# Routing table by 0/1 products and weights by gathers without repeats in the expert stage of a one-core layer kernel

## The chip, the core and the metric

The kernel runs on one core of one Trainium2 chip. The metric is the device time in microseconds of one execution, lower is better. The engines of a core are TensorE (PE; its weight loads are PEld), VectorE (DVE), ScalarE (ACT), GpSimd (POOL) and SyncE (SP, which here only issues DMAs). Each has its own instruction queue, and semaphores tie them together. Sixteen DMA engines serve the transfers that SP, ACT and POOL issue.

## What is computed

One layer of a hybrid backbone: modulated norm, two token mixers (mLSTM and gated linear attention) on one input projection, a gated merge, and then a mixture of experts over the 1024 latent tokens of width 1024. The change touches the mixture of experts and one line of the first stage. Cut to that part, the reference is:

```python
def hier_moe(h, w_grp, b_grp, w_rexp, b_rexp, w_up, w_down):
    p_grp = softmax(hf @ w_grp + b_grp); grp_p, grp = top_k(p_grp, 1)          # 4 groups
    e_logits = (hf @ w_rexp + b_rexp).reshape(n_tok, 4, 4)
    p_in = softmax(e_logits[arange(n_tok), grp[:, 0]]); top_p, top_i = top_k(p_in, 2)
    weights = grp_p * top_p / sum(top_p)
    expert = grp * 4 + top_i                                                   # 2 of 16 experts a token
    # assignments sorted by expert, each expert's segment padded to 128 rows
    ...
    def expert_block(xb, e):                                                   # xb: 128 x 1024
        gate, up = split(xb @ w_up[e], 2)                                      # w_up[e]: 1024 x (512 + 512)
        return (silu(gate) * up) @ w_down[e]                                   # w_down[e]: 512 x 1024
    # y[token] += weight * row
```

All arithmetic is float32; the kernel reaches that precision by splitting each operand into a high part in float32r and a low part, and forming three products (high x high, high x low, low x high). Two choices of 1024 tokens are 2048 assignments, padded to at most 31 blocks of 128 rows (BLOCKS = 31), always all computed; blocks that no expert needs use expert 15's weights.

## The kernel before

The program runs stages one after the other; each stage is a block of instructions for the five engines that ends when all of them have. The last four are `mix_out` (projections, second norm, router logits), `route`, `experts` and `combine`.

`route` is mostly one chain on VectorE in which each operation waits for the one before (`then`). It waits for the router's bias (loaded by SP at its start), finds group and experts, their weights, and the place of each assignment: `dest_i`, block x 128 + rank. TensorE helps with two products for prefix sums. From the token counts it derives the number of blocks of each expert (L2296 to L2298) and the expert of each block, `block_e` (L2302 to L2305). Last it computes `place_i`, where each assignment's token number belongs in a table in DRAM, `row_token` (L2318 to L2320), which SP has filled with zeros.

`experts` begins on GpSimd with 16 scatters of 128 words into that table (L2401), its load back into SBUF (L2405), and from there one gather of 128 rows of x for each block (L2414), whose indices are copied from the table first (L2411). SP meanwhile loads the weights: for each block three pieces of 2 MB, piece 0 the gate half of `w_up` (512 of its 1024 columns), piece 1 the up half, piece 2 `w_down`. The expert is read from `block_e` into a register, and all 31 blocks load all three. Each piece has one buffer in `ex_raw`, free when its low part is done.

For every block, ScalarE copies a piece to its high part `ex_w_hi` in two halves (L2477) and VectorE subtracts to get `ex_w_lo` (L2517), both one block ahead for pieces 0 and 1. TensorE multiplies the block's x (transposed by L2433, split by L2481 and L2522) with piece 0 into `ex_g_ps` and with piece 1 into `ex_u_ps` (L2424 to L2426, 24 products each), transposes the next x, does the down product of the block before, and transposes the hidden values (L2464). ScalarE's Silu is L2495, VectorE's gate product L2532, the hidden halves L2539 and L2541; ScalarE empties the down product (L2487) and stores it (L2489). The loop over blocks is a hardware loop over pairs, with the first two and the last written out.

The contraction runs over `(k p)`: chunk k of 128 takes x columns 128k to 128k+127.

`combine` gathers the two rows of each token and adds them. It is not touched.

## Time and profile before

| | us |
|---|---|
| median of 3 runs | 2668.78 (2663.82 to 2674.18) |
| the profiled execution, whole | 2670.58 |
| its span, first to last instruction | 2668.6 |
| routing, first to last VectorE operation | 1914.33 to 1931.98 |
| first expert product on TensorE | 1968.95 |
| Silu of first and of last block | 1976.8, 2570.2 |
| combine, to the end | 2601.8 to 2668.6 |

All times in the rows are microseconds from the start of the span, in one profiled execution. A row of the timeline gives the start, the duration, the engine, the line of the kernel, the operation with output and inputs, how many instructions were merged in it (x8), and in brackets how long the engine had been idle before it and who released it. A duration of a single matmul includes its way through the array; how fast products follow each other is seen from their starts.

### The profile page before, as it was taken

Reading aid. Unit: us, or ns where it says so; the run is one execution under the profiler, and the core shown is the slowest. Engines: PE = TensorE matmul, PEld = TensorE weight load, DVE = VectorE, ACT = ScalarE, POOL = GpSimd, SP = SyncE. Lnnn points to the kernel's source line nnn. Section 1 sums busy time; section 2 is a strip of 40 time slices with the busy share of each in tenths; the row PEclk is TensorE's granted clock in tenths of the full one; section 3 lists DMA queues with packets and bytes.
Section 4 is the critical chain, followed back from the end, with each engine's and each line's share of the span. In section 5 each row is a group of like instructions: output and inputs, shape, how many; then the busy total and the mean of one; then the engine's idle time right before and its main releaser. Section 6 shows DMA issues by size and latency. Waiting matters only on the chain. (4 is left out here: it accounts for less than half of the span.)

```text
span 2668.6 us, 28745 instructions
## 1 busy us (share of the span) xinstructions
PE 2264.5 (85%) x10734; PEld 1822.7 (68%) x10734; DVE 1417.7 (53%) x1723; ACT 1053.4 (39%) x1302; POOL 773.0 (29%) x571
## 2 busy tenths in 40 slices
PE   6989979993999995799999689999349999999970
PEld 1278868872888884688888567777337777777760
DVE  1435631104323222779887445433348888888856
ACT  1322201111234333354554434422136666766643
POOL 5300001000346443466766322200132112111105
PEclk9989989995999996899999889999569999999995
DMA  7633252113444555233354466552279999999956
GB/s 274 216 74 91 74 199 86 49 48 135 130 143 143 142 141 164 75 125 113 118 134 114 126 212 193 179 161 84 75 272 360 373 377 360 374 371 359 374 192 267
DMA packets 325269, 500.12 MB, mean 187 GB/s; under 512 B 22102, under 2 KB 171750, under 8 KB 324524
## 3 DMA queue, kind: packets, MB, share of 16 engines
q1 hardware_dynamic: 306156, 433.65, 48.0%
q0 software_dynamic: 12816, 43.55, 5.5%
q10 hardware_dynamic: 6192, 21.51, 2.0%
q8 instruction: 68, 1.11, 0.2%
q14 instruction: 37, 0.30, 0.0%
HBM read 409.96 MB, written 88.69 MB: 187 GB/s over the span
## 5 line engine op out<-in xcount | busy, mean ns | idle before, releaser
L2517 DVE TENSOR_TENSOR ex_w_lo<-ex_raw,ex_w_hi 128x2048 fp32r<-128x2048 f32 x186 | 417.8, 2288 | 115.3 <-ACT ex_w_hi L2477 113.3
L2477 ACT ACTIVATE ex_w_hi<-ex_raw 128x2048 fp32r<-128x2048 f32 x186 | 345.8, 1908 | 92.0 <-DMA ex_raw<-in_w_up_dram 51.8
L666 POOL DMA_DIRECT2D vals<-rows_stage x40 | 21.8, 546 | 438.8 <-ACT rows_stage L658 438.8
L2411 POOL COPY ex_idx<-ex_rows 128x1 int32 (+1 forms) x31 | 20.9, 675 | 434.6 <-PE ex_x_ps L2433 433.1
L2424 PE MATMUL ex_g_ps<-ex_w_hi,ex_x_hi 128*128 128x512 f32 x248 | 104.5, 422 | 42.6 <-DVE ex_x_lo L2522 42.6
L1527 PEld LDWEIGHTS gl_lv_ps<-gl_q_level,gl_k_level 128*128 128x128 f32 x896 | 108.3, 194 | 10.5 <-issue 5.6
L1992 DVE TENSOR_TENSOR mo_w_lo<-mo_w,mo_w_hi 128x1024 fp32r<-128x1024 f32 x48 | 59.8, 1245 | 100.7 <-ACT mo_w_hi L1889 100.7
L878 PE MATMUL gl_u_ps<-half_hi,gl_u_w_hi 128*128 128x512 f32 x256 | 110.3, 431 | 3.4 <-ACT gl_u_exp L896 3.4
L1527 PE MATMUL gl_lv_ps<-gl_q_level,gl_k_level 128*128 128x64 f32 x896 | 111.0, 276 | 2.3 <-DVE gl_scores L1657 1.5
L2103 PE MATMUL mo_ps<-mo_branch_hi,mo_w_hi 128*128 128x512 f32 x256 | 105.4, 412 | 6.4 <-DVE mo_w_lo L1992 5.9
L878 PE MATMUL ml_u_ps<-half_hi,ml_u_w_hi 128*128 128x512 f32 x256 | 104.0, 406 | 8.0 <-ACT ml_u_exp L896 8.0
L658 ACT ACTIVATE rows_stage<-rows_ps 128x512 f32<-128x512 f32 x40 | 23.9, 598 | 211.7 <-PE rows_ps L635 211.7
L2424 PE MATMUL ex_y_ps<-ex_w_hi,ex_hidden_hi 128*128 128x512 f32 x248 | 100.7, 406 | 7.6 <-DVE ex_w_lo L2517 7.6
L879 PE MATMUL gl_u_ps<-half_lo,gl_u_w_hi 128*128 128x512 f32 x256 | 103.5, 404 | 0.0
L2104 PE MATMUL mo_ps<-mo_branch_hi,mo_w_lo 128*128 128x512 f32 x256 | 103.2, 403 | 0.0
L880 PE MATMUL gl_u_ps<-half_hi,gl_u_w_lo 128*128 128x512 f32 x256 | 103.1, 403 | 0.0
L2105 PE MATMUL mo_ps<-mo_branch_lo,mo_w_hi 128*128 128x512 f32 x256 | 102.8, 402 | 0.0
L879 PE MATMUL ml_u_ps<-half_lo,ml_u_w_hi 128*128 128x512 f32 x256 | 101.5, 396 | 0.0
L2425 PE MATMUL ex_g_ps<-ex_w_lo,ex_x_hi 128*128 128x512 f32 x248 | 101.3, 409 | 0.0
L880 PE MATMUL ml_u_ps<-half_hi,ml_u_w_lo 128*128 128x512 f32 x256 | 101.3, 396 | 0.0
L2426 PE MATMUL ex_g_ps<-ex_w_hi,ex_x_lo 128*128 128x512 f32 x248 | 101.1, 408 | 0.0
L2426 PE MATMUL ex_y_ps<-ex_w_hi,ex_hidden_lo 128*128 128x512 f32 x248 | 99.6, 402 | 0.0
(378 smaller groups left out, 6181.6 us busy)
## 6 DMA issues: line engine op xcount, KB each, us to landing
ex_raw<-in_w_up_dram SPq DMA_DIRECT2D x62, 2048.0 KB, 12.7
ex_raw<-in_w_down_dram SPq DMA_DIRECT2D x31, 2048.0 KB, 9.9
fr_w<-in_w_mod_dram SPq DMA_DIRECT2D x12, 2048.0 KB, 10.0
ml_u_w<-in_w_in_dram SPq DMA_DIRECT2D x32, 512.0 KB, 5.6
gl_u_w<-in_w_in_dram SPq DMA_DIRECT2D x32, 512.0 KB, 5.1
expert_rows<-ex_y ACTq DMA_DIRECT2D x31, 512.0 KB, 7.4
vals<-rows_stage POOLq DMA_DIRECT2D x40, 256.0 KB, 2.3
ml_v<-vals SPq DMA_DIRECT2D x20, 512.0 KB, 3.9
```

Source lines behind the costliest of these rows:

```text
L878: pe.matmul(self.ps[:, :], a_hi, b_hi, start=(k == 0), stop=False)
L879: pe.matmul(self.ps[:, :], a_hi, b_lo, start=False, stop=False)
L880: last = pe.matmul(self.ps[:, :], a_lo, b_hi, start=False, stop=(k == KD - 1))
L1527: last = pe.matmul(lv_ps[at_l // 2 % 2][:, lv_cols(at_l, h)], kl[:, d, l, h * P:(h + 1) * P], ql[:, l, h * P // 2:(h + 1) * P // 2], start ...
L2103: pe.matmul(out, a_hi, b_hi_, start=(k == 0), stop=False)
L2104: pe.matmul(out, a_lo, b_hi_, start=False, stop=False)
L2105: last = pe.matmul(out, a_hi, b_lo_, start=False, stop=(k == KD - 1))
L2424: pe.matmul(dst, a_hi[:, ka], hi[:, q, at:at + 512], start=first, stop=False)
L2425: pe.matmul(dst, a_hi[:, ka], lo[:, q, at:at + 512], start=False, stop=False)
L2426: return pe.matmul(dst, a_lo[:, ka], hi[:, q, at:at + 512], start=False, stop=last)
L2477: act.activation(hi[:, q, h], raw[:, q, h], ACT.Copy).then_inc(hi_done[q], 1)
L2517: dve.tensor_tensor(lo[:, q, at], raw[:, q, at], hi[:, q, at].bitcast(F32), ALU.subtract)\
```

## The change

It has four parts.

The table. `route` keeps `dest_i`, but instead of a table in DRAM it builds it in SBUF: for each of the two choices and each of 8 columns of tokens it forms two 0/1 tiles, `rt_is_rank` (128 tokens x 128 ranks) and `rt_in_block` (128 tokens x 32 blocks, times the token number), and 16 products in one accumulation give `m.table`, rank x block. The scatters, their table in DRAM and `place_i` are gone. Each expert now has at least one block, so that block 0 is always expert 0's. The number of blocks comes from an add and a shift. The router bias is loaded in the first stage, `constants`.

The first block. Since it is expert 0's, SP loads its three pieces at the start of `route`, and ScalarE makes the high halves of pieces 0 and 1 there. The weight buffers are placed before `route` for that.

The gathers. All later weights are fetched by GpSimd's indirect DMA, with one row of 16 KB per partition. The row numbers `m.w_rows` hold, for each block and piece, expert x 256 + 2 x partition (+ 1) or expert x 128 + partition; where the expert is that of the block before, 2^20 is added, which is outside the bound and is skipped, so that `ex_raw` keeps what it has. The splitting into high and low parts is done for every block as before.

The pieces. A gathered row holds whole rows of the matrix, so piece 0 is now the first 4 of each 8 rows of `w_up` with all 1024 columns (gate and up), piece 1 the other 4. Each piece feeds both `ex_g_ps` and `ex_u_ps`, and the gate is complete when 36 of 48 products are done (`g_made`). x is transposed by columns that lie 8 apart and the hidden values by columns 4 apart. ScalarE splits piece 0 ahead of the Silu, and makes `ex_x_hi` ahead of piece 1; VectorE makes `ex_x_lo` ahead of piece 1. The loop is written out for all 31 blocks.

```diff
-            then(ts(blocks[:, :], pre[:, N, :], 0.0, None, ALU.is_gt))
-            for q in range(1, SEQ // P):
-                then(dve.scalar_tensor_tensor(out=blocks[:, :], in0=pre[:, N, :], scalar=float(P * q),
-                                              in1=blocks[:, :], op0=ALU.is_gt, op1=ALU.add))
+            then(ts(count_i[:, :], pre[:, N, :], float(P - 1), None, ALU.add))
+            then(ts(count_i[:, :], count_i[:, :], 7, None, ALU.logical_shift_right))
+            then(ts(blocks[:, :], count_i[:, :], 1.0, None, ALU.max))
...
+            up = w["w_up"][0][0].rearrange("(p h k) n -> h p (k n)", h=2, k=KD // 2)
+            down = w["w_down"][0][0].rearrange("(p k) n -> p (k n)", k=FF // P)
+            for q, src in enumerate((up[0], up[1], down)):
+                sp.dma_start(raw[:, q, :], src).then_inc(first[q], 16)
+            sp.wait_ge(first[2], 16)
...
+            for k in range(TOP_K):
+                pe.wait_ge(places, k + 1)
+                for n in range(N):
+                    last = pe.matmul(table_ps[:, :], is_rank[:, k, n, :], in_block[:, k, n, :],
+                                     start=(k == 0 and n == 0), stop=(k == TOP_K - 1 and n == N - 1))
+            last.then_inc(tables, 1)
...
+            then(ts(where_i[:, 0], m.dest_i[:, :, :], P - 1, None, ALU.bitwise_and))
+            then(ts(where_i[:, 1], m.dest_i[:, :, :], 7, None, ALU.logical_shift_right))
+            then(dve.tensor_copy(where[:, :, :, :], where_i[:, :, :, :]))
...
+            for k in range(TOP_K):
+                then(tt(hit[:, k], wide(where[:, 1, k, :], WIDE), along(which[:, :], WIDE), ALU.is_equal))
+                then(tt(in_block[:, k], hit[:, k], wide(token[:, :], WIDE), ALU.mult))
+                tt(is_rank[:, k, :, :], wide(where[:, 0, k, :], P), along(rank[:, :], P), ALU.is_equal)\
+                    .then_inc(places, 1)
+            dve.wait_ge(tables, 1)
+            then(dve.tensor_copy(m.table[:, :], table_ps[:, 0:BLOCKS]))
...
+            then(tt(again[:, 1:], blk[:, 1:], blk[:, 0:BLOCKS - 1], ALU.is_equal))
+            then(ts(again[:, :], again[:, :], float(SKIP), None, ALU.mult))
+            for q, rows in enumerate((2 * P, 2 * P, P)):
+                if q != 1:
+                    then(dve.scalar_tensor_tensor(out=row0[:, :], in0=blk[:, :], scalar=float(rows), in1=again[:, :],
+                                                  op0=ALU.mult, op1=ALU.add))
+                then(ts(m.w_rows[:, q, :], row0[:, :], part[:, q:q + 1], None, ALU.add))
...
-            def load(b, q):
-                e = sp.value_load(m.block_e[0:1, bass.ds(b, 1)], min_val=0, max_val=EXPERTS - 1)
...
+                pool.wait_ge(lo_done[q], 2 * b)
+                rows = EXPERTS * P * (1 if q == 2 else 2)
+                pool.indirect_dma_start(out=raw[:, q, :], out_offset=None, in_=sources[q],
+                                        in_offset=bass.IndirectOffsetOnAxis(ap=m.w_rows[:, q, b:b + 1], axis=0),
+                                        bounds_check=rows - 1, oob_is_err=False).then_inc(loaded[q], 16)
...
+                by_chunk = xg[:, j, :].rearrange("p (c k) -> p k c", k=KD)
                 for k in range(KD):
-                    last = pe.transpose(x_ps[:, k * P:(k + 1) * P], xg[:, j, k * P:(k + 1) * P], m.ident[:, :])
+                    last = pe.transpose(x_ps[:, k * P:(k + 1) * P], by_chunk[:, k, :], m.ident[:, :])
...
             def step(b, j, half):
-                act.wait_ge(made[0], b + 1)
+                if more(b):
+                    split_hi(b + 1, 0)
+                act.wait_ge(s["g_made"], b + 1)
...
                 if more(b):
-                    split_hi(b + 1, 0)
+                    x_hi(b + 1)
                     split_hi(b + 1, 1)
-                    x_hi(b + 1)
...
                 if more(b):
+                    x_lo(b + 1)
                     split_lo(b + 1, 1)
-                    x_lo(b + 1)
```

How instructions stand on an engine, in the words of the built programs (line, operation, output from inputs, shape, how many in a row). First VectorE in one block of the expert stage, before:

```order
L2517 TENSOR_TENSOR ex_w_lo<-ex_raw,ex_w_hi 128x2048 x4
L2532 TENSOR_TENSOR ex_hidden<-ex_u_ps,ex_gate 128x512
L2517 TENSOR_TENSOR ex_w_lo<-ex_raw,ex_w_hi 128x2048 x2
L2522 TENSOR_TENSOR ex_x_lo<-ex_x_ps,ex_x_hi 128x1024
L2539 CAST ex_hidden_hi<-ex_h_ps 128x512
L2541 TENSOR_TENSOR ex_hidden_lo<-ex_h_ps,ex_hidden_hi 128x512
```

And after; of the four subtractions in the first row, two are the third piece of the block before and two the first piece of the next block:

```order
L2549 TENSOR_TENSOR ex_w_lo<-ex_raw,ex_w_hi 128x2048 x4
L2564 TENSOR_TENSOR ex_hidden<-ex_u_ps,ex_gate 128x512
L2554 TENSOR_TENSOR ex_x_lo<-ex_x_ps,ex_x_hi 128x1024
L2549 TENSOR_TENSOR ex_w_lo<-ex_raw,ex_w_hi 128x2048 x2
L2571 CAST ex_hidden_hi<-ex_h_ps 128x512
L2573 TENSOR_TENSOR ex_hidden_lo<-ex_h_ps,ex_hidden_hi 128x512
```

The low half of x has moved ahead of the subtraction of the second piece. Next ScalarE in one block, before, from the Silu on:

```order
L2495 ACTIVATE ex_gate<-ex_g_ps 128x512
L2477 ACTIVATE ex_w_hi<-ex_raw 128x2048 x4
L2481 ACTIVATE ex_x_hi<-ex_x_ps 128x1024
L2487 ACTIVATE ex_y<-ex_y_ps 128x1024
L2489 DMA expert_rows<-ex_y 128x1024
L2477 ACTIVATE ex_w_hi<-ex_raw 128x2048 x2
```

And after:

```order
L2530 ACTIVATE ex_gate<-ex_g_ps 128x512
L2514 ACTIVATE ex_x_hi<-ex_x_ps 128x1024
L2510 ACTIVATE ex_w_hi<-ex_raw 128x2048 x2
L2520 ACTIVATE ex_y<-ex_y_ps 128x1024
L2522 DMA expert_rows<-ex_y 128x1024
L2510 ACTIVATE ex_w_hi<-ex_raw 128x2048 x4
```

The first piece's high half now stands ahead of the Silu (the last two of the four at the end), and x between the Silu and the second piece. Last GpSimd, from the start of the expert stage, before:

```order
L2401 DMA row_token<-token,place_i 4096x1 x16
L2405 DMA ex_rows<-row_token 128x32
L2411 COPY ex_idx<-ex_rows 128x1
L2414 DMA ex_x<-moe_in,ex_idx 128x1024
L2411 COPY ex_idx<-ex_rows 128x1
L2414 DMA ex_x<-moe_in,ex_idx 128x1024
```

And after (the pattern of four repeats from there for each block):

```order
L2432 DMA ex_x<-moe_in,table 128x1024 x2
L2425 DMA ex_raw<-in_w_up_dram,w_rows 128x4096
L2425 DMA ex_raw<-in_w_up_dram,w_rows 128x4096
L2432 DMA ex_x<-moe_in,table 128x1024
L2425 DMA ex_raw<-in_w_up_dram,w_rows 128x4096
L2425 DMA ex_raw<-in_w_up_dram,w_rows 128x4096
L2425 DMA ex_raw<-in_w_down_dram,w_rows 128x4096
L2432 DMA ex_x<-moe_in,table 128x1024
```

The scatters and the copies of indices are gone, and the weight fetches, which SP issued before, stand in GpSimd's queue between the gathers of x.

## Rows read from the trace of the kernel before

**Rows 1.** The page, part 1: busy time of each engine, share of the span.
```profile
PE 2264.5 (85%) x10734; PEld 1822.7 (68%) x10734; DVE 1417.7 (53%) x1723; ACT 1053.4 (39%) x1302; POOL 773.0 (29%) x571
```

**Rows 2.** Stretches: length, busy of PE, PEld, DVE, ACT, POOL, clock, DMA share, GB/s.
```profile
2200.00:2300.00 100.00, 92.93 (x420) 74.62 (x419) 83.23 (x51) 68.89 (x46) 18.87 (x11) 0.98 0.99 366
```

**Rows 3.** Timeline, routing: start, duration, engine, line, operation, idle time before.
```profile
1911.62 0.43 SPq L2206 DMA_DIRECT2D rt_bias<-in_b_rexp_dram  x1
1914.33 0.33 DVE L2246 TENSOR_TENSOR rt_lg<-logits,rt_bias 128x160 f32<-128x160 f32 x1 [3.60 <-DMA rt_bias<-in_b_rexp_dram]
...
1925.90 1.43 DVE L2298 SCALAR_TENSOR_TENSOR rt_blocks<-rt_pre,rt_blocks 128x16 f32<-128x16 f32 x7
...
1927.59 0.68 DVE L2302 TENSOR_TENSOR rt_le<-rt_ends,rt_which 128x496 f32<-128x496 f32 x1
...
1931.81 0.17 DVE L2320 CUSTOM_DVE_ANT_0 place_i<-place_i,rt_hi 128x32 uint16<-128x32 uint16 x1
```

**Rows 4.** Timeline, start of the expert stage.
```profile
1933.23 1.11 POOL L2401 DMA_INDIRECT row_token<-token,place_i  x1 [21.50 <-POOLq L2164]
...
1954.22 0.96 POOL L2401 DMA_INDIRECT row_token<-token,place_i  x1 [0.30 <-issue]
...
1960.03 1.02 POOL L2414 DMA_INDIRECT ex_x<-moe_in,ex_idx  x1 [0.83 <-POOL ex_idx L2411]
...
1964.62 1.97 PE L2433 MATMUL ex_x_ps<-ident,ex_x 128*128 128x128 f32 x8 [41.16 <-DMA ex_x<-moe_in,ex_idx]
...
1967.68 1.22 DVE L2522 TENSOR_TENSOR ex_x_lo<-ex_x_ps,ex_x_hi 128x1024 fp32r<-128x1024 f32 x1 [19.65 <-ACT ex_x_hi L2481]
...
1968.95 0.80 PE L2424 MATMUL ex_g_ps<-ex_w_hi,ex_x_hi 128*128 128x512 f32 x1 [2.37 <-DVE ex_x_lo L2522]
```

**Rows 5.** The Silu of every block (L2495): all 31 in one row; then two neighbours.
```profile
L2495 ACT ACTIVATE ex_gate<-ex_g_ps x31: 598/598/602, 1976.8 to 2570.2; 128x512 f32<-128x512 f32 x31
...
1997.69 0.60 ACT L2495 ACTIVATE ex_gate<-ex_g_ps 128x512 f32<-128x512 f32 x1 [6.97 <-PE ex_g_ps L2426]
2016.96 0.60 ACT L2495 ACTIVATE ex_gate<-ex_g_ps 128x512 f32<-128x512 f32 x1 [1.96 <-PE ex_g_ps L2426]
```

**Rows 6.** Timeline of one block, TensorE, ScalarE and VectorE.
```profile
2214.60 0.39 PE L2424 MATMUL ex_u_ps<-ex_w_hi,ex_x_hi 128*128 128x512 f32 x1
...
2216.93 0.39 PE L2425 MATMUL ex_u_ps<-ex_w_lo,ex_x_hi 128*128 128x512 f32 x1
...
2220.20 1.04 PE L2433 MATMUL ex_x_ps<-ident,ex_x 128*128 128x128 f32 x8
2226.67 0.60 PE L2464 MATMUL ex_h_ps<-ident,ex_hidden 128*128 128x128 f32 x4
2228.16 0.49 PE L2424 MATMUL ex_g_ps<-ex_w_hi,ex_x_hi 128*128 128x512 f32 x1 [0.90 <-DVE ex_x_lo L2522]
...
2220.45 3.72 ACT L2477 ACTIVATE ex_w_hi<-ex_raw 128x2048 fp32r<-128x2048 f32 x2 [1.45 <-PE ex_u_ps L2426]
...
2226.82 1.22 DVE L2522 TENSOR_TENSOR ex_x_lo<-ex_x_ps,ex_x_hi 128x1024 fp32r<-128x1024 f32 x1
```

**Rows 7.** Timeline of the same block: GpSimd's gather and VectorE's subtractions beside it.
```profile
2222.55 2.98 POOL L2414 DMA_INDIRECT ex_x<-moe_in,ex_idx  x1 [0.79 <-POOL ex_idx L2411]
...
2222.40 4.49 DVE L2517 TENSOR_TENSOR ex_w_lo<-ex_raw,ex_w_hi 128x2048 fp32r<-128x2048 f32 x2
```

**Rows 8.** DMA, 2000 to 2500; then one weight load of 1936 to 1954 (us to landing).
```profile
DMA packets 72598, 184.35 MB, mean 369 GB/s; under 512 B 2000, under 2 KB 2000, under 8 KB 72595
...
ex_raw<-in_w_up_dram SPq DMA_DIRECT2D x50, 2048.0 KB, 13.0
...
ex_raw<-in_w_up_dram SPq DMA_DIRECT2D x1, 2048.0 KB, 7.9
```

**Rows 9.** Timeline, routing: two reductions, of elements 4 apart and of neighbours.
```profile
1916.90 0.37 DVE L2268 TENSOR_REDUCE rt_es<-rt_sel 128x32 f32<-128x128 f32 x1
...
1930.73 0.42 DVE L2315 TENSOR_REDUCE rt_dest<-rt_prod 128x16 f32<-128x256 f32 x1
```

More of the change, by code:

```diff
@@ L2351, in experts @@
         s = {name: sem(f"ex_{name}") for name in (
-            "table", "idx", "t_x", "x_hi", "x_lo", "gate", "hidden", "t_h", "h_hi", "h_lo", "y_left",
-            "gather_begun")}
-        loaded, hi_done, lo_done, made = ([sem(f"ex_{n}{q}") for q in range(3)] for n in (
-            "loaded", "hi_done", "lo_done", "made"))
-        scattered = sem("ex_scattered")
+            "t_x", "x_hi", "x_lo", "g_made", "gate", "hidden", "t_h", "h_hi", "h_lo", "y_left")}
+        loaded, made = ([sem(f"ex_{n}{q}") for q in range(3)] for n in ("loaded", "made"))
@@ L2365, in each @@
[L2365 to L2388 removed]
+            for b in range(BLOCKS):
+                body(b, b % 2, b // 2)
@@ new lines, in experts, with _, gather @@
+        late = lambda b, n: b >= n
+        more = lambda b: b < BLOCKS - 1
+        @block.gpsimd
+        def _(pool):
+            def load(b, q):
+                pool.wait_ge(lo_done[q], 2 * b)
[3 more added lines that the diff above has]
+                                        bounds_check=rows - 1, oob_is_err=False).then_inc(loaded[q], 16)
+            def gather(b):
+                if b >= 2:
+                    pool.wait_ge(s["t_x"], b - 1)
+                pool.indirect_dma_start(out=xg[:, b % 2, :], out_offset=None, in_=m.h2,
+                                        in_offset=bass.IndirectOffsetOnAxis(ap=table[:, b:b + 1], axis=0))\
+                    .then_inc(gathered[b % 2], 16)
+            gather(0)
+            gather(1)
+            for b in range(BLOCKS):
+                if b + 1 < BLOCKS:
@@ L2419, in _ @@
+                if b:
+                    load(b, 2)
+                if b + 2 < BLOCKS:
+                    gather(b + 2)
         @block.tensor
@@ L2735, in build @@
         if upto >= 4:
-            run(route, experts, combine)
+            with ExitStack() as moe:
+                m.ex_raw = place(moe, "ex_raw", [P, 3, KD // 2 * D])
+                m.ex_hi = place(moe, "ex_w_hi", [P, 3, KD // 2 * D], F32R)
+                m.ex_lo = place(moe, "ex_w_lo", [P, 3, KD // 2 * D], F32R)
+                run(route, experts)
+            run(combine)
 _INS = ["x", "c", "ctx", "c_ctx", "w_mod", "b_mod", "g_norm1", "w_in", "ml_conv", "ml_conv_b", "b_mgate", "ml_norm",
```

172 lines of the change are left out of this document (76 added, 96 removed).

## The prediction

> **What bounds the kernel now.** I read the page first: TensorE is busy 85% of the span, far ahead of VectorE's 53% [rows 1]. That average says little about the two stages that the change touches, so next came the stretches and the order of time inside them.
>
> The expert stage takes about 630 us. In a stretch of it TensorE is busy 93 us of 100, VectorE 83, ScalarE 69, and the 16 DMA engines show a share of 0.99 at 366 GB/s [rows 2]: everything is near its limit. Which wait ends last? The gate activations mark the blocks: the first at 1976.8, the last at 2570.2 [rows 5], 593.4 us for 30 steps, a mean of 19.78. The shortest step is 19.27 (1997.69 to 2016.96) [rows 5] and returns often. Its anatomy stands in [rows 6]: the gate and up products end when the transposes start at 2220.20; ScalarE then splits the second weight piece (3.72), VectorE subtracts behind it, and only at 2226.82 does it reach the low half of x (1.22), which TensorE waits for until 2228.16, idle 0.90 us. So 19.27 is a loop of dependences; TensorE alone would need less. What makes the mean 0.5 us longer is the weights: 75 weight loads of 2 MB and 25 blocks' rows in and out are 184.35 MB in 500 us, 369 GB/s [rows 8], 7.34 MB a block, which at that rate is 19.9 us. Two limits lie on each other.
>
> Ahead of it is a hole. VectorE starts routing at 1914.33 after a wait of 3.60 us for the bias [rows 3], ends it at 1931.98, and TensorE's first expert product starts at 1968.95 [rows 4]. Between them GpSimd issues 16 scatters of one word a row (1933.23 to 1955.2), loads the table, gathers x (1960.03), and x is transposed from 1964.62 [rows 4]. No weight is awaited there.
>
> **The change part by part.** *Start of the expert stage.* The bias is loaded in the first stage instead, so VectorE starts at about 1911.2: 3.1 off. The seven comparisons of 1.43 us and the first one become three small operations of some 0.21: 1.0 off. The three operations behind the destination go: 0.6 off. The expert of each block (from 1927.59, 1.6 us) moves behind the table [rows 3]. The destination is thus known at 1925.6 instead of 1931.35. Added: three small operations (0.6); for each of two choices two operations of 256 elements (0.43, between the 0.33 of 160 and the 0.68 of 496) and one of 1024 (1.22, as x_lo in [rows 4]), 4.2 in all; then 8 more products of 32 columns and their hand-off, 1.9 us (bounds 0.8 and 2.2); the table's copy, the block experts and seven small operations for the weight rows, 3.3. Routing ends at 1935.6. From the last routing operation to GpSimd's first took 1.25 us (1931.98 to 1933.23), so the gather of x is issued at 1936.9. Before, it was 4.6 us from issue to transpose (1960.03 to 1964.62) and 4.35 from there to the product [rows 4]. But now VectorE subtracts two SBUF tiles at that moment, and beside such a subtraction a gather took 2.98 us [rows 7] against 1.02 [rows 4]; I add 1.9. First product: 1936.9 + 6.5 + 4.35 = 1947.7, **21.2 us earlier** (19 to 23). The 6 MB of block 0 and the hi halves of its up pieces need about 18 us of DMA and 7.4 of ScalarE, hidden behind 24 us of routing; SP only waits there. Two more small loads on SP in the first stage come behind six others while TensorE still transposes: nothing, 0.5 at worst.
>
> *Less to load.* From the reference's inputs I worked out the tokens per expert: experts 0 to 7 and 12 to 15 have one block each, 8 to 11 have 3, 3, 4, 3. That is 25 blocks; the 6 unused ones repeat expert 15. So 15 of 31 blocks repeat the expert before and fetch no weights, and 16 do (block 0 in routing). A repeat needs 1.05 MB instead of 7.34, so DMA leaves its path. Of the 15 others, 8 (blocks 1 to 8) and 4 (21 to 24) follow each other and stay bound by DMA; 11, 14 and 18 stand alone, and a slot is free for some 12 us before it is needed, against 7.9 for one load that runs alone [rows 8] and 1 to 3 us of GpSimd: hidden.
>
> *x_lo ahead of the second piece.* The x halves need only the x transposes. TensorE's own work is 72 products at a start-to-start of 0.233 us (2214.60 to 2216.93 is ten) = 16.8, plus 1.04 and 0.60 for the transposes [rows 6]: 18.45. What is late next? The second piece is split while the first is multiplied: its low half is done 19.9 us after the products' start and needed at 18.45 + 5.6 = 24. VectorE's row (three pieces at 4.49 [rows 7], 1.22, three of 0.7) is 16.8 us in 18.45: I find 0.3 us of slack. With hand-offs 18.6.
>
> *Strided transposes.* Row halves need x columns 8 apart and hidden columns 4 apart. No TensorE row here reads columns apart. Bounds: zero, and the nearest row, on VectorE: a reduction of 128 elements that lie 4 apart took 0.37 us, one of 256 side by side 0.42 [rows 9]. With 0.16 of fixed cost that is 1.64 ns an element against 1.02, 1.6 times. A transpose takes 0.130 (1.04/8); 1.6 times 0.14 of load is +0.085. Twelve a block: 0 to +1.0 us. That row is another engine's, and the loading of one tile overlaps the passing of the last, so I take the middle, +0.5: pace 19.1.
>
> *Issue by GpSimd.* Four indirect DMAs a block at 1.0 to 3.0 us each are 4 to 12 us of GpSimd in 19. They are queued in one order: next block's two up pieces, this block's down, x. Behind a waiting load stand only loads that come free later, and x, which has over 10 us. A gather of 16 KB rows is not in this trace; skipped rows neither. I take 1 to 3 us for both.
>
> **The sum.** Block 0 to 1 has no down product before it: 13.2 (products: the gate came 7.6 after their start at half of them [rows 4, 5], plus 24 x 0.233) + 1.1 + 1.0 + 1.2 + hand-offs = 17.3. Eleven steps at DMA's pace, 19.8. Eighteen at 19.1. Together 17.3 + 217.8 + 343.8 = 578.9, against 593.4: **14.5 off**. The last block's tail and the combine stage stay. 21.2 + 14.5 = 35.7. The profiled execution had a span of 2668.6 within 2670.6 us; the new one 2632.9 within 2634.9. The median of the runs was 1.8 below the profiled one: **2633**.
>
> **The rivals.** *A, strides are free:* 18 steps at 18.6, 9 off more: 2624. For it: no TensorE row shows such a cost, and the next tile is loaded while the last one passes.
>
> *B, strides cost the full 0.085:* pace 19.6, 9 more than my sum, and 1 at the start: 2643. The Trainium skill speaks for it (Advanced Engine Details and Errata, SBUF Cachelines): a line is 16 bytes, and an access pattern that touches another line each time pays a penalty. It names no size for TensorE; by it both strided reads pay, and the time would be near 2643. VectorE's row agrees; no run here yet shows TensorE's.
>
> *C, GpSimd's issue makes loads late:* each slot is then free for 3 us less, and the eleven steps take 21.5: +19, 2652. For it: before, two loads were queued back to back and the queue never ran dry [rows 2, 8]. Against it: slots take 6.5 (split) + 3 + 7.9 = 17.4 under 19.8.
>
> *D, slower:* a fetch of rows four times as long costs GpSimd four times 0.96, and 2 to 2.7 of waiting for VectorE: about 6.5. Three and a gather are 22.5 us in every block, whether skipped or not, and GpSimd becomes the bound: 30 x 22.5 = 675, 81.6 more, minus 21.2: 2729. It turns into a loss from 20.5 us a block, 5.8 a fetch. Against it: a scatter of 128 words took as long (0.96) as a gather of 128 rows of 4 KB (1.02) [rows 4], so rows count and not bytes.
>
> The other direction of the same port: VectorE could be held by the four issues. The pair of subtractions beside the gather took 4.49, as any other [rows 7]. The Trainium skill (SBUF — State Buffer, SBUF: two separate sides) says that whoever of the two starts first holds the pair of ports for its whole instruction and the other fully blocks. By that rule VectorE would lose up to 1 us four times a block and the pace would be near 21; the row shows GpSimd waiting and VectorE not, so this stays inside D's chance.
>
> **How the numbers follow.** Forecast 0.35, A 0.27, B 0.20, C 0.10, D 0.08. The predicted time is 2633. D is left out of the range, and a tenth for the far ends; from A minus its uncertainties (start 2, the eleven steps faster by 1 us each if long rows load better) to C plus some: 2608 to 2658. A measurement of this kernel tells 0.5%, 13 us, from no change. Faster by more (below 2655.4): forecast, A, B and two thirds of C with a reserve, 0.84; within: 0.09; slower: 0.07.
>
> **What the profile of the changed kernel would show.** The first expert product 19 to 23 us earlier; no scatters. DMA share near 1 only in blocks 1 to 8 and about 21 to 24, low elsewhere, and some 101 MB of expert weights instead of 195. Steps between gates of 18.5 to 19.2 in repeats (18.6 says A, 19.6 B), eight x transposes in 1.04 (A) or up to 1.7 (B). x_lo ahead of the subtraction of the second piece, and TensorE's wait before a block's first product gone. GpSimd's issues at 1 to 3 us (D: 6). I would be wrong if TensorE waits for the first or second piece in repeats (VectorE's 0.3 us of slack gone), or for late weights in the first eight blocks.

## The result, and the profile after

| | before | after |
|---|---|---|
| median of 4 runs, us | 2671.48 (2663.82 to 2681.14) | 2597.13 (2587.59 to 2600.56) |
| ratio, 95% interval | | 0.9714 (0.9671 to 0.9758) |
| profiled execution: whole, span | 2670.6, 2668.6 | 2594.0, 2592.3 |
| first expert product of block 0 | 1968.95 | 1946.66 |
| first expert product of block 30 | 2564.33 | 2488.33 |
| mean step between blocks | 19.85 | 18.06 |

The change is 2.9% faster. The forecast was 2633 with a range from 2608 to 2658: the direction was right, and the time is 11 us below the range. The two spans differ by 76.3 us: 22.3 lie ahead of the first expert product, 53.7 in the 30 steps between blocks (595.38 against 541.67), and 0.3 behind them. Forecast were 21.2, 14.5 and 0, so the whole miss is in the steps. The DMA packets carry 94 MB less than the 500.12 MB of before, as forecast (101 MB of expert weights in place of 195).

The page of after, part 1 (busy time, share of the span, instructions), and the total of the DMA packets. They answer [rows 1]:

```profile
PE 2247.4 (87%) x10750; PEld 1827.3 (70%) x10750; DVE 1417.2 (55%) x1732; ACT 1051.2 (41%) x1302; POOL 815.1 (31%) x616
...
DMA packets 257150, 406.08 MB, mean 157 GB/s; under 512 B 27190, under 2 KB 176822, under 8 KB 250236
```

The busy times of TensorE, VectorE and ScalarE have hardly moved; the same work stands closer together. Stretches of after, with the columns of [rows 2] (length, busy of PE, PEld, DVE, ACT, POOL, clock, DMA share, GB/s):

```profile
2000.00:2100.00 100.00, 95.27 (x437) 77.50 (x438) 86.98 (x55) 71.31 (x49) 20.58 (x21) 1.00 0.98 382
2200.00:2300.00 100.00, 100.00 (x473) 83.81 (x472) 94.32 (x59) 78.36 (x52) 32.10 (x22) 1.00 0.41 147
...
2230.67:2248.41 17.74, 17.74 (x86) 14.87 (x85) 16.86 (x11) 13.57 (x10) 6.57 (x5) 1.00 0.18 59
```

The first line is a stretch in which weights are still fetched for every block, the second one with repeated experts, where TensorE has no gap left. The third is one repeating block from Silu to Silu: 17.74 us, all of them TensorE's.

The start of the expert stage in after's timeline (start, duration, engine, line, operation, idle time and its releaser), to be read against [rows 3, 4]:

```profile
1910.41 0.32 DVE L2281 TENSOR_TENSOR rt_lg<-logits,router_bias 128x160 f32<-128x160 f32 x1 [0.54 <-PEq L1710]
...
1934.93 0.24 DVE L2371 TENSOR_SCALAR w_rows<-rt_row,rt_part 128x31 int32<-128x31 f32 x1
...
1936.42 2.54 POOL L2432 DMA_INDIRECT ex_x<-moe_in,table  x1 [25.22 <-SPq L2381]
...
1942.32 1.97 PE L2461 MATMUL ex_x_ps<-ident,ex_x 128*128 128x128 f32 x8 [10.72 <-DMA ex_x<-moe_in,table]
...
1946.66 0.79 PE L2451 MATMUL ex_g_ps<-ex_w_hi,ex_x_hi 128*128 128x512 f32 x1 [2.37 <-DVE ex_x_lo L2554]
```

Routing ends at 1935.2 (forecast 1935.6), the gather of x is issued at 1936.42 (1936.9) and takes 2.54 beside VectorE's subtraction, and the first product comes at 1946.66 (1947.7). A part of this closeness is chance: in v0_after, the same kernel, routing begins at 1913.27 and the first product comes at 1949.77, since the stages ahead of routing do not take the same time in every execution.

One repeating block of after on TensorE, ScalarE, VectorE and GpSimd, to be read against [rows 6, 7]:

```profile
2232.22 1.04 PE L2461 MATMUL ex_x_ps<-ident,ex_x 128*128 128x128 f32 x8
...
2233.02 0.48 PE L2451 MATMUL ex_y_ps<-ex_w_hi,ex_hidden_hi 128*128 128x512 f32 x1
...
2233.30 1.03 ACT L2514 ACTIVATE ex_x_hi<-ex_x_ps 128x1024 fp32r<-128x1024 f32 x1 [2.06 <-PE ex_x_ps L2461]
...
2234.36 1.23 DVE L2554 TENSOR_TENSOR ex_x_lo<-ex_x_ps,ex_x_hi 128x1024 fp32r<-128x1024 f32 x1
...
2234.96 0.99 POOL L2425 DMA_INDIRECT ex_raw<-in_w_up_dram,w_rows  x1 [0.30 <-issue]
...
2236.16 4.49 DVE L2549 TENSOR_TENSOR ex_w_lo<-ex_raw,ex_w_hi 128x2048 fp32r<-128x2048 f32 x2 [0.58 <-ACT ex_w_hi L2510]
...
2238.58 0.63 PE L2497 MATMUL ex_h_ps<-ident,ex_hidden 128*128 128x128 f32 x4
...
2238.97 0.48 PE L2451 MATMUL ex_g_ps<-ex_w_hi,ex_x_hi 128*128 128x512 f32 x1
```

The low half of x is ready at 2235.59, 3.4 us before the product that needs it (2238.97), where before TensorE waited for it at 2228.16. And look at the starts: the eight x transposes take 0.80 us of TensorE's time (2232.22 to 2233.02), though their row says 1.04, since the end of the last one lies beside the next product. The four hidden transposes take 0.39 (2238.58 to 2238.97), not 0.63.

### The profile page after: what moved, and what is told of

It reads as the page before. It is cut to its first block and busy times, and to the rows that moved or that the text cites. A ratio compares the mean times of both kernels' runs of the same rounds, so it can differ in the third digit from the quotient of the medians.

```text
span 2592.3 us, 27681 instructions
## 1 busy us (share of the span) xinstructions
PE 2247.4 (87%) x10750; PEld 1827.3 (70%) x10750; DVE 1417.2 (55%) x1732; ACT 1051.2 (41%) x1302; POOL 815.1 (31%) x616
## 5 line engine op out<-in xcount | busy, mean ns | idle before, releaser
L2549 DVE TENSOR_TENSOR ex_w_lo<-ex_raw,ex_w_hi 128x2048 fp32r<-128x2048 f32 x186 | 416.5, 2285 | 52.3 <-ACT ex_w_hi L2510 47.4
L2510 ACT ACTIVATE ex_w_hi<-ex_raw 128x2048 fp32r<-128x2048 f32 x182 | 337.9, 1908 | 94.9 <-DMA ex_raw<-in_w_up_dram,w_rows 55.0
L2425 POOL DMA_INDIRECT ex_raw<-in_w_up_dram,w_rows x60 | 60.8, 1013 | 222.9 <-DVE ex_w_lo L2549 215.4
L2425 POOL DMA_INDIRECT ex_raw<-in_w_down_dram,w_rows x30 | 52.9, 1764 | 161.8 <-DVE ex_w_lo L2549 161.8
L905 POOL TENSOR_SCALAR ml_u_exp<-ml_u_exp 128x512 f32<-128x512 f32 x32 | 61.5, 1921 | 132.9 <-ACT ml_u_exp L900 132.8
L2452 PE MATMUL ex_y_ps<-ex_w_lo,ex_hidden_hi 128*128 128x512 f32 x248 | 98.0, 395 | 0.0
```

What stands on the lines that cost most here:

```text
L2425: pool.indirect_dma_start(out=raw[:, q, :], out_offset=None, in_=sources[q], in_offset=bass.IndirectOffsetOnAxis(ap=m.w_rows[:, q, b:b + 1 ...
L2452: pe.matmul(dst, a_hi[:, ka], lo[:, q, at:at + 512], start=False, stop=False)
L2510: act.activation(hi[:, q, h], raw[:, q, h], ACT.Copy).then_inc(hi_done[q], 1)
L2549: dve.tensor_tensor(lo[:, q, at], raw[:, q, at], hi[:, q, at].bitcast(F32), ALU.subtract)\
```

## The experiments

The theory after this comparison: TensorE's own work is the bound of a step, the x halves' place in the order was what held it before, and DMA was not the limit of before that its share of 0.99 suggested. The rivals: skipping the repeats brought the steps down, or the products themselves became faster. I give each run its mean step from the first product of block 0 to that of block 30, read from TensorE's timeline, as for the two kernels above (19.85 and 18.06). Ratios are to the kernel before on the same chip.

**The order of the x halves alone.** Once taken back in after, once put alone into before:

```diff
 # u1_x_behind: after, ScalarE; VectorE likewise
-                    x_hi(b + 1)
                     split_hi(b + 1, 1)
+                    x_hi(b + 1)
 # u4_before_x_ahead: before, ScalarE; VectorE likewise
                     split_hi(b + 1, 0)
+                    x_hi(b + 1)
                     split_hi(b + 1, 1)
-                    x_hi(b + 1)
```

> The kernel after with one part undone: on ScalarE and VectorE the halves of the next x stand behind the second weight piece again. Theory O (the order is worth what the prediction said): TensorE then waits for x_lo before each block's first product as before; the chain from the end of the up products is one half split, the pair of subtractions and x_lo, some 7.9 us, against 7.0 of TensorE's own work, so a repeat step is 18.6 to 18.7 instead of 17.75: 22 to 28 us slower in the stage. Rival (VectorE has room elsewhere and TensorE does not wait): within 3 us of the kernel after.

> The kernel before with one part of the change alone: x_hi and x_lo of the next block ahead of the second weight piece. Theory D (DMA is the second limit right behind it): the shortest step falls from 19.27 to some 18.3, but the mean only from 19.85 to about 19.7, since 7.34 MB a block at 369 to 380 GB/s take 19.3 to 19.9; 0 to 8 us faster. Rival (the order alone is worth 1 us a block): 25 to 30 us faster.

Measured: after without the order 2631.37, ratio 0.9856 (0.9839 to 0.9872), mean step 19.21, repeats at 18.91 to 18.95. Before with it 2638.34, ratio 0.9873 (0.9857 to 0.989), mean step 18.63. So the order is worth 34 us in the one (medians) and 34 (1.27%; 32 by the medians) in the other. Both are more than was expected before the runs: 22 to 28 in the first, and in the second 0 to 8, with 25 to 30 as the rival. Waits of u1_x_behind from 2000 to 2490 (engine and line, what it waited for, us in total, times, longest): the old wait of TensorE is back, once a block.

```profile
PE ex_g_ps L2451 <- DVE ex_x_lo L2554: 25.7, 26, 2.0
```

In after the same row holds 2.7 us. The stretch 2000 to 2490 of before, of u4_before_x_ahead and of u1_x_behind, in this order:

```profile
2000.00:2490.00 490.00, 459.60 (x2083) 369.13 (x2083) 409.77 (x249) 338.52 (x224) 91.76 (x50) 0.99 0.99 368
```

```profile
2000.00:2490.00 490.00, 480.63 (x2200) 386.08 (x2199) 427.27 (x262) 354.51 (x236) 81.33 (x54) 1.00 1.02 393
```

```profile
2000.00:2490.00 490.00, 464.34 (x2159) 385.03 (x2158) 424.19 (x258) 348.93 (x231) 133.76 (x103) 1.00 0.58 218
```

The first two lines are the key of this case. The same loads through the same queue show a DMA share of 0.99 at 368 GB/s and of 1.02 at 393, and all that differs is when x is split. The transfers of before were paced by the buffers that came free, not the other way round. ScalarE's wait for the up weights in the same stretch, first in before, then in u4_before_x_ahead, says the same:

```profile
ACT ex_w_hi L2477 <- DMA ex_raw<-in_w_up_dram: 26.7, 25, 1.5
```

```profile
ACT ex_w_hi L2477 <- DMA ex_raw<-in_w_up_dram: 100.6, 52, 5.4
```

ScalarE stands waiting for weights 1.1 us a block in before and 3.9 once the order is changed. The mean step lies 0.5 to 0.6 above the shortest ones in both (19.85 against 19.27, 18.63 against 18.12), so late weights may well add this much in either; what falls with the order is the step below it. The third shows the converse: with a share of 0.58 the loop of x alone still costs 18.9 us a block.

**Skipping.** All 31 blocks fetched with the same gathers; fetched by SP in the same whole rows, 16 KB from each partition, with nothing skipped; and nothing fetched behind block 0:

```diff
 # s3_no_skip
-            then(ts(again[:, :], again[:, :], float(SKIP), None, ALU.mult))
+            then(ts(again[:, :], again[:, :], 0.0, None, ALU.mult))
 # u2_sp_rows: on SP, in place of GpSimd's indirect DMA
+                e = sp.value_load(m.block_e[0:1, b:b + 1], min_val=0, max_val=EXPERTS - 1)
...
+                    src = w["w_up"][0][bass.ds(e, 1)].rearrange("a (p h k) n -> p h (a k) n", h=2, k=KQ)[:, q]
...
+                sp.dma_start(raw[:, q, :].rearrange("p (k n) -> p k n", n=D), src).then_inc(loaded[q], 16)
 # u3_no_fetch
-                if b + 1 < BLOCKS:
-                    load(b + 1, 0)
-                    load(b + 1, 1)
-                if b:
-                    load(b, 2)
```

> The kernel after with the repeats fetched too (2^20 is not added to their row numbers), so all 31 blocks fetch 6.3 MB by GpSimd's gathers. Theory D (skipping is what frees the path, and a fetching block runs at the pace of DMA): every step between first products is 18.9 to 19.1 us, as in blocks 2 to 8 of the kernel after, so 22 steps lose 1.2 to 1.3 us: 27 us slower, about 2624. Theory Q (long rows in one queue are fetched faster, and the pace would be near 17.75 with or without skipping): within 5 us of the kernel after. Theory K (the old pace of 19.8 comes back): 45 us slower.

> The kernel after with the same 16 KB rows loaded by SP (expert number read into a register) for all 31 blocks instead of by GpSimd's gathers, nothing skipped. It is to be compared with the run that gathers all 31 blocks without skipping, whose steps had a mean of 18.66 us and whose DMA moved 386 to 397 GB/s, against 369 in the kernel before. Theory R (whole rows of 16 KB are what raises the rate; the queue does not matter): mean step 18.5 to 18.8, over 385 GB/s. Theory G (the gathers' own queue raises the rate): mean step near 19.5 and 370 GB/s.

> The kernel after without any weight fetch behind block 0; all blocks use expert 0's weights. (This leaves the fetches and so the right result out.) It prices what the 15 remaining fetches still cost. In the kernel after, the steps of blocks 2 to 8 are 17.77, 20.61, 19.05, 18.97, 19.15, 18.85 and 18.68 instead of 17.75, together 8.8 us, and blocks 23 and 24 lose 0.8. Theory: all steps behind the first at 17.75, so the stage is 9.6 us shorter than in the kernel after. Rival (VectorE or ScalarE still stretch some steps): less than 5 us.

| | median, us | ratio | mean step |
|---|---|---|---|
| after | 2597.13 | 0.9714 (0.9671 to 0.9758) | 18.06 |
| s3_no_skip | 2613.83 | 0.9781 (0.9752 to 0.981) | 18.66 |
| u2_sp_rows | 2589.66 | 0.9691 (0.967 to 0.9711) | 17.78 |
| u3_no_fetch | 2584.71 | 0.9674 (0.9658 to 0.969) | 17.74 |

The stretch 2000 to 2490 of s3_no_skip, of u2_sp_rows, of u3_no_fetch:

```profile
2000.00:2490.00 490.00, 473.90 (x2192) 388.41 (x2190) 428.14 (x263) 352.93 (x237) 123.46 (x105) 1.00 0.99 393
```

```profile
2000.00:2490.00 490.00, 489.72 (x2311) 410.27 (x2310) 452.00 (x279) 372.78 (x248) 50.34 (x25) 1.00 0.99 407
```

```profile
2000.00:2490.00 490.00, 490.00 (x2318) 410.82 (x2317) 458.87 (x278) 374.52 (x248) 24.15 (x26) 1.00 0.16 59
```

Without any fetch a step is 17.74; with every weight fetched by SP it is 17.78, at 407 GB/s. So at this pace DMA is no bound at all, if the rows are long and SP issues them; ScalarE still waits 83.9 us in 47 times for up weights in u2_sp_rows, which costs TensorE next to nothing. GpSimd's gathers of the same rows stay at 393 GB/s and cost 0.9 us a step. Skipping thus gives back what the gathers take (17 us with them) and brings nothing that SP's own loads would not have had: u2_sp_rows, which skips nothing, is no slower than after, by the medians 7 us faster. Of what was expected, only u3_no_fetch came as written (its 30 steps are 9.6 us shorter than after's). s3_no_skip was to lose 27 us or less than 5 and lost 17, and u2_sp_rows was to have a step of 18.5 or more. Whether the gathers lose through their late issue or through their descriptors was not separated. Which part of 407 against u4's 393 the row length gives was not tried alone either.

**Strides.** The transposes of after on adjoining columns, here for x and in the same way for the hidden values; this leaves out the reordering of the contraction:

```diff
-                by_chunk = xg[:, j, :].rearrange("p (c k) -> p k c", k=KD)
+                by_chunk = xg[:, j, :].rearrange("p (k c) -> p k c", k=KD)
```

> The kernel after with the x and hidden values transposed by neighbouring columns, as before, instead of columns 8 and 4 apart. (This leaves the reordering of the contraction out.) Theory A (strides are free on TensorE): no change within 2 us, and eight x transposes stay at 1.04 us and 0.80 us to the next product. Theory B (strides cost): 31 x up to 1 us faster.

Measured: 2594.81, ratio 0.9716 (0.9687 to 0.9745), repeats at 17.73 against 17.75. The x transposes of 2100 to 2220, first of s4_plain_turns, then of after (count, busy time, mean ns, idle time ahead):

```profile
L2461 PE MATMUL ex_x_ps<-ident,ex_x 128*128 128x128 f32 x56 | 7.2, 272 | 0.0
```

```profile
L2461 PE MATMUL ex_x_ps<-ident,ex_x 128*128 128x128 f32 x56 | 7.3, 273 | 0.0
```

The weight loads of the same transposes, in the same order:

```profile
L2461 PEld LDWEIGHTS ex_x_ps<-ident,ex_x 128*128 128x128 f32 x56 | 6.5, 140 | 0.9
```

```profile
L2461 PEld LDWEIGHTS ex_x_ps<-ident,ex_x 128*128 128x128 f32 x56 | 7.3, 188 | 0.6
```

Columns 8 apart do lengthen the load of a tile, from 140 to 188 ns (those of the hidden values, 4 apart, from 139 to 204), but nearly all of it lies beside the passing of the tile before: from start to start eight x transposes take 0.80 us against 0.79 and four hidden ones 0.39 against some 0.36. The repeat step pays 0.02 us for the strides.

**The spacing of the products.** From start to start, products of 512 columns take 0.2334 us in before and 0.2274 in after (mean of 2100 to 2220; the up products' rows read 394 to 397 and 389 to 390 ns). In before two small tiles lie between the weights' tiles and those of x; after has none. In s1_rows_last they are placed last in before; the others put an unused tile of so many bytes a partition there in after (s2_pad_x: two, of 128 and 8 bytes, as before had them; its expectation calls them some 160):

```diff
 # s1_rows_last: before
-        table = sb("ex_rows", [P, BLOCKS + 1], I32)
-        idx = sb("ex_idx", [P, 2], I32)
...
         yo = sb("ex_y", [P, 2, D])
+        table = sb("ex_rows", [P, BLOCKS + 1], I32)
+        idx = sb("ex_idx", [P, 2], I32)
 # s5_pad32: after
+        pad = sb("ex_pad", [P, 8])
         xg = sb("ex_x", [P, 2, D])
```

> The kernel before with one thing changed: the two small tiles ex_rows and ex_idx (some 160 bytes of each partition) are placed behind all other tiles of the expert stage instead of in front of ex_x, so that the x and hidden tiles lie, relative to the weight tiles, as in the kernel after. Question: why do the 128x512 products of the expert stage start every 0.2335 us before and every 0.2275 us after? Theory P (placement of the tiles in a partition): the spacing falls from 0.2335 towards 0.2275, 72 products a block save up to 0.43 us, and the stage, bound partly by DMA, gives 3 to 13 us. Theory L (the written-out loop or the order of the columns does it): spacing stays at 0.2335 and the time at that of the kernel before.

> The kernel after with two unused small tiles (some 160 bytes of each partition) in front of ex_x, as before had ex_rows and ex_idx there. Theory P (placement): the spacing of the products goes back to 0.2335 and the run is 9 to 13 us slower than the kernel after (31 blocks x 0.43). Theory L: spacing 0.2275 and the time of the kernel after.

> The kernel after with an unused tile of 32 bytes a partition in front of ex_x. 160 bytes there took the spacing of the products from 0.2274 to 0.2332 us. Theory P32 (what matters is the place within a line of 64 bytes or so): spacing 0.233 again. Theory P128 (only the 128 bytes of it mattered): 0.2274.

> The changed kernel with one unused tile of 64 bytes a partition between the weight tiles and the x tile. Theory (the products' spacing follows where the tiles lie against a grid of 64 bytes or finer): spacing 0.2275 us as without the tile, repeat steps 17.75, span near 2592. Rival (only the place without any tile is fast, or the grid is coarser than 64 bytes): 0.2332 and steps near 18.16, as the tile of 32 bytes gave, span near 2596.

> The same with 96 bytes, which is 32 beyond a multiple of 64. Theory of a 64-byte grid: 0.2332, steps near 18.16. Rival (a shift is slow up to some size and then harmless, or a coarser grid of which 96 is a fast place): 0.2275, steps 17.75.

> The same with 128 bytes. Theory of a 64-byte grid: 0.2275, steps 17.75, span near 2592. A grid of 128 bytes gives the same here and 0.2332 with the tile of 64 bytes. Rival (no grid: any tile between them is slow): 0.2332 and 18.16.

> The changed kernel with an unused tile of 2048 bytes a partition between the weight tiles and the x tile. 2048 bytes is the size of one moving tile of 512 columns. Theory (fast when x and weights lie a multiple of 2048 bytes apart, whatever comes ahead of both): spacing 0.2275 us, repeat steps 17.75. Rival (only directly adjoining tiles are fast): 0.2332 and 18.16.

> The same with 512 bytes, the size of one loaded tile of 128 columns. Theory of multiples of 2048 bytes: 0.2332, steps near 18.16. A grid of 512 bytes: 0.2275, 17.75.

> The changed kernel with an unused tile of 256 bytes a partition between the weight tiles and the x tile. 512 and 2048 bytes left the spacing at 0.2274 us, 32, 64, 96, 128 and 160 made it 0.2329 to 0.2341. Theory (multiples of 512 bytes): 0.2332, repeat steps 18.16. Rival (multiples of 256 bytes): 0.2274, 17.75.

| between weights and x | spacing, us | repeat step | time, us |
|---|---|---|---|
| after, nothing | 0.2274 | 17.75 | 2597.13 |
| 32 bytes | 0.2332 | 18.16 | 2597.48 (one run) |
| 64 | 0.2332 | 18.17 | 2603.58 (one run) |
| 96 | 0.2341 | 18.22 | 2609.21 (one run) |
| 128 | 0.2329 | 18.15 | 2602.99 (one run) |
| 128 and 8 | 0.2332 | 18.15 | 2602.70, ratio 0.9741 (0.9713 to 0.9768) |
| 256 | 0.2274 | 17.75 | 2591.51 (one run) |
| 512 | 0.2274 | 17.75 | 2592.62 (one run) |
| 2048 | 0.2274 | 17.75 | 2593.17 (one run) |
| before, rows and indices moved | 0.2272 | | 2671.05, ratio 0.9983 (0.9965 to 1.0001) |

The up products in one stretch (2100 to 2220) of s7_pad96 and of s11_pad256:

```profile
L2452 PE MATMUL ex_u_ps<-ex_w_hi,ex_x_hi 128*128 128x512 f32 x52 | 20.6, 396 | 0.0
```

```profile
L2452 PE MATMUL ex_u_ps<-ex_w_hi,ex_x_hi 128*128 128x512 f32 x55 | 21.4, 389 | 0.0
```

So the grid of 64 bytes that I had guessed for the first of these runs fell, and so did 128, 2048 and, last, 512: all distances tried that are a multiple of 256 bytes are fast, all others slow, by 2.4 to 2.9%. The spacing and the repeat step are what to compare. The times of single runs also hold what the stages ahead took (the first operation of routing comes at 1917.47 in s7_pad96 and at 1910.41 in after), and s2_pad_x lost 6 us where 9 to 13 were expected. Is it the address of x that matters, or its distance from the weights? u2_sp_rows and v1_combined, made for other questions, place one more tile of 124 bytes (`block_e`) ahead of both the weights and x, and their spacing is 0.2275: x moved by as much as in s8_pad128 (0.2329), but the weights moved with it. So it is the distance that matters in these runs; why it does stays open. In s1_rows_last the faster products moved the time by no more than can be told: there the loop of x sets the step. In after they set it.

**Together.** u5_both has in before the order of x and the moved tiles:

> The kernel before with two parts: x_hi and x_lo ahead of the second weight piece, and the two small tiles placed last. Weights still by SP in rows of 2 and 4 KB, all blocks. With the order alone the mean step was 18.63 us and the shortest 18.12, DMA moved 393 GB/s. Theory R (rows of 2 and 4 KB reach no more than about 393 GB/s): shortest step 17.72, but the mean stays at 18.6. Rival (the rate was only what the pace asked for, and row length does not matter): mean 17.9 to 18.2, as the run with SP's 16 KB rows had 17.78 at 407 GB/s.

Measured: 2628.29, ratio 0.9854 (0.9828 to 0.988), mean step 18.28; its steps alternate between 17.7 and some 19. Its stretch:

```profile
2000.00:2490.00 490.00, 479.07 (x2244) 393.12 (x2243) 436.45 (x269) 362.15 (x242) 90.08 (x54) 1.00 1.03 399
```

The mean step was expected either to stay at 18.6 or to lie between 17.9 and 18.2, and lies between the two. The 7.34 MB of a block at 399 GB/s are 18.4 us, which is near the step: with the products this fast and rows of 2 to 4 KB, DMA may well be the limit, at 399 GB/s and not at 369. That is not shown. ScalarE waits for up weights 97.9 us in 53 times, but it did so in u4_before_x_ahead as long (100.6), and the run with long rows differs from this one in the division of the pieces too.

v1_combined is u2_sp_rows without the computation of `w_rows` in routing, with every down product waiting for one half of its low weights at a time (which can matter for the last block's), and with the first subtraction held back until GpSimd has begun its gather. It ran beside after itself (v0_after):

```diff
-                pe.wait_ge(lo_done[2], 2 * b + 2)
+                pe.wait_ge(lo_done[2], 2 * b + 1)
...
+                for half in range(2):
+                    if half:
+                        pe.wait_ge(lo_done[2], 2 * b + 2)
...
-            for q, rows in enumerate((2 * P, 2 * P, P)):
...
             gather(0)
+            pool.sem_inc(s["begun"], 1)
             gather(1)
```

> A version made of what the runs showed: the kernel after, but SP loads all 31 blocks by whole rows of 16 KB, nothing skipped (2589.7 us in its own run); the seven small operations for row numbers go from routing (1.4 us); VectorE starts its first subtraction only when GpSimd has issued the first gather, so that this takes 1.0 instead of 2.5 us; and the down product waits for the second half of its weights only in its middle, which matters for the last block, where TensorE stood idle 7.5 us (2.2 us less, and up to 1.7 more if its clock holds). Theory: 5 to 7 us below the run with SP's loads, so about 2584, and 10 to 14 us below the kernel after. Rival (none of the three small parts is on the path): 2590.

> The kernel after, unchanged, beside the combined version on the same chip, so that the two can be compared. Expected: 2597 us within 5, steps of 17.75 in repeats.

Measured: 2585.82, ratio 0.9681 (0.9659 to 0.9704), against 2596.02, ratio 0.9731 (0.971 to 0.9752): 10 us faster than after, as expected (10 to 14), the best of the runs that fetch their weights, and by the medians 4 us below u2_sp_rows where 5 to 7 were expected. Its steps are 17.73 in the mean. TensorE's wait ahead of the last down product, first in after, then in v1_combined:

```profile
2512.94 0.79 PE L2451 MATMUL ex_y_ps<-ex_w_hi,ex_hidden_hi 128*128 128x512 f32 x1 [7.54 <-DVE ex_w_lo L2549]
```

```profile
2504.25 0.79 PE L2443 MATMUL ex_y_ps<-ex_w_hi,ex_hidden_hi 128*128 128x512 f32 x1 [5.33 <-DVE ex_w_lo L2544]
```

The half-wise wait starts them 2.2 us sooner. The third edit did not shorten the gather: these are the subtraction and the gather of v1_combined,

```profile
1938.87 4.49 DVE L2544 TENSOR_TENSOR ex_w_lo<-ex_raw,ex_w_hi 128x2048 fp32r<-128x2048 f32 x2 [1.06 <-POOLq L2432]
1939.05 3.06 POOL L2428 DMA_INDIRECT ex_x<-moe_in,table  x1 [23.74 <-POOLq L2170]
```

the signal behind the gather let VectorE go 0.18 us before the gather's work began, and that took 3.06 as beside any subtraction.

## Why the prediction was wrong in its size

**The start** was right: 22.3 us against 21.2. Of these 0.8 came from stages ahead of routing (its first operation at 1910.4 where 1911.2 was taken), which is chance: it came between 1909.2 and 1917.5 in the profiles of after and its variants. Counted from that operation, each later step was within 0.6: the end of routing, the issue, its 2.54 beside the subtraction for a forecast of 2.9.

**The count of repeats** was right: steps of 17.75 without a wait for weights, and a low DMA share, where repeats were forecast.

**"Eleven steps at DMA's pace, 19.8"** failed. They took 17.77, 20.61, 19.05, 18.97, 19.15, 18.85, 18.68 (blocks 1 to 8) and 17.76, 17.75, 17.92, 18.38 (21 to 24): 204.9 us for a forecast of 217.8, 13 too many. The sentence behind it is "Two limits lie on each other": a share of 0.99 at 369 GB/s was read as DMA's limit. u4_before_x_ahead carried 393 with the same loads, u2_sp_rows 407. A share near 1 was measured at 368, 393, 399 and 407 GB/s, so it says that something is always in flight, not how much more would fit. What in before's own rows could have told this: TensorE waited for x_lo at the shortest steps [rows 6], and the loop was long enough without DMA. The stretch 2340 to 2380 of after already moves 397 GB/s, over 7% above "DMA's pace":

```profile
2340.00:2380.00 40.00, 40.00 (x189) 33.39 (x188) 33.82 (x22) 28.91 (x20) 11.80 (x9) 1.00 0.99 397
```

**"Eighteen at 19.1"** was the larger miss: 17.75, so 24 us. It has three parts. The strides, +0.5 a block, cost 0.02: 9 us. The working had put 1.6 times on the load of a tile; the load became 1.3 to 1.5 times as long, but nearly all of it is hidden. The transposes were entered with their busy times (1.04 and 0.60) in place of the distance of the starts (0.80 and 0.39), which counted the tail of the last one twice: 0.45 a block, 8 us. The spacing of 0.233 was taken over from before, where it was 0.2274 after: 0.4 a block, 7 us. s2_pad_x agrees with that size, its 30 steps are 6.1 us longer than after's. No view of before told that moving two small tiles would do this.

**x_lo ahead of the second piece**: the mechanism was right (the wait of 0.90 [rows 6] is gone, and u1_x_behind brings it back), and "what is late next" was right too: nothing on VectorE, whose 0.3 us of slack held, with 16.86 busy of 17.74. But its price stood nowhere alone in the sum. With DMA's pace put in for eleven blocks, the order had been given a gain only in the others; the runs show that it is worth 32 to 34 us, more than any other single part of the change, also without any skipping.

**Of the rivals**, A (strides free) was the true case for its term, and even its 18.6 was 0.85 too long. B fell with s4_plain_turns. The Trainium skill (Advanced Engine Details and Errata, SBUF Cachelines) puts a penalty on patterns that touch another line of 16 bytes each time; the loads of TensorE's transposes agree with it in direction (188 against 140 ns), the transposes themselves hardly show it (273 against 272 ns), VectorE's reduction [rows 9] may. C and D fell on their sizes, though C's mechanism is there in small: the gathers cost 0.9 us a step against SP's loads. Of the signs that were named for being wrong, a wait for pieces in repeats did not come. Late weights in the first eight blocks did (u3_no_fetch has 17.75 there), but only one of those steps is above the 19.8 that was taken for them. The repeats lie below the forecast 18.5 to 19.2 without any such sign. GpSimd's issues in after, all of the stage (count, busy us, mean ns, idle time):

```profile
L2425 POOL DMA_INDIRECT ex_raw<-in_w_up_dram,w_rows x60 | 60.8, 1013 | 222.9 <-DVE ex_w_lo L2549 215.4 <-issue 7.5
...
L2432 POOL DMA_INDIRECT ex_x<-moe_in,table x31 | 54.1, 1745 | 34.4 <-SPq L2381 25.2 <-issue 6.7 <-PE ex_x_ps L2461 2.4
L2425 POOL DMA_INDIRECT ex_raw<-in_w_down_dram,w_rows x30 | 52.9, 1764 | 161.8 <-DVE ex_w_lo L2549 161.8
```

A fetch of 128 rows of 16 KB takes 1.01 us, as one of 4 KB [rows 4]: the bytes do not count. That the rows do was argued in the prediction, and no run has a fetch with another number of rows. And the port went the way the row had shown: GpSimd's issue is stretched to as much as 3.06 us when a subtraction runs, while the subtraction stays at 4.49 for two, with four issues a block as with one. The gather of 1936.42 begins 0.71 us into a subtraction of 2.24 and takes 2.54, which is the 1.53 that are left of it and the usual 1.0. The other way round, in after:

```profile
2007.36 0.99 POOL L2425 DMA_INDIRECT ex_raw<-in_w_up_dram,w_rows  x1 [5.14 <-DVE ex_w_lo L2549]
2007.82 4.48 DVE L2549 TENSOR_TENSOR ex_w_lo<-ex_raw,ex_w_hi 128x2048 fp32r<-128x2048 f32 x2
```

Here GpSimd began first, and the subtraction neither waited nor took longer. The rule of the Trainium skill (SBUF — State Buffer, SBUF: two separate sides), that whoever starts first fully blocks the other, fits the first case and not the second. (It names a VectorE operation with two SBUF inputs against a GpSimd operation that reads SBUF; what GpSimd reads during an issue no view here shows.)

With all terms as measured, the sum of the steps is 17.2 + 204.9 + 319.6 = 541.7, for 578.9 forecast. One small slip remains: the forecast set its sum, which counts from first product to first product, against 593.4, which counts from Silu to Silu; between the products it was 595.4, and the gain is 53.7 where the terms alone give 51.7.

## What to carry to other kernels

A DMA share near 1 is no proof of a DMA limit where buffers are reused: ask first which dependence frees the buffer, and test it by moving that one alone, before paying for a scheme that moves fewer bytes. Cost pipelined work by the distance of the starts in the timeline, never by busy times, whose tails lie beside the next instruction. When a change moves tiles in SBUF, allow for a few per cent on TensorE in either direction, and try operands a multiple of 256 bytes apart.

## What the runs showed of the hardware that was not expected

- Where the tiles lie sets the pace of float32r products of 512 columns: 0.2274 us when the distance between weights and x was 0, 256, 512 or 2048 bytes, 0.2329 to 0.2341 when it was 32, 64, 96, 128 or some 136. A tile placed ahead of both changed nothing (0.2275).
- Loads of tiles whose columns lie 8 or 4 apart take 188 and 204 ns in place of 140, and the transposes that use them follow each other as before.
- The 16 DMA engines show a share of 0.99 at 368 GB/s and at 407. SP's loads of 16 KB rows carried 407 GB/s at TensorE's pace of 17.78 a block, without a sign of a limit; GpSimd's gathers of the same rows stayed at 393.
- A skipped fetch costs GpSimd as much as one that moves 2 MB: 2230.67 to 2248.41 in after moves 59 GB/s, just x in and out, and its three fetches still take 1 to 2.4 us each.
- Two-input subtractions on VectorE lengthen GpSimd's indirect DMA issues (from 1.0 up to 3.1 us, by what is left of the running subtraction) and are not lengthened by them (2285 ns each with four issues a block, 2288 with one).
